# A hybrid decoder step on one core: the opening's transposes, weight splits and gate matmuls rearranged, and the sample state decayed by one ScalarE pass

## The reference

```python
h = rmsnorm(x, norm1_g)
z = h @ w_in                                   # 2048 x 16400
u, cg, bg, q, k, v, o, gif, g_a, g_b = split(z)
conv_out, sc = causal_dwconv(cg * u, sc0, w_shortconv)
a_out = bg * conv_out
gif = gif + b_if                               # 16 columns: 8 input gates, 8 forget gates
ig, lf = gif[:, :H], log_sigmoid(gif[:, H:])
hb, (c, n, m) = mlstm_sequence(qh, kh, vh, ig, lf, state0, first)
b_out = sigmoid(o) * hb
x = x + (sigmoid(g_a) * a_out + sigmoid(g_b) * b_out) @ w_out
up, fc = causal_dwconv(rmsnorm(x, norm2_g) @ w_up, fc0, w_ffconv)
x = x + (silu(up[..., D_FF:]) * up[..., :D_FF]) @ w_down
# for each sample row, in mlstm_chunk:
c_new = carry * c_prev + g * outer(k, v)       # 128 x 256 for each of 8 heads
```

## Time and profile before

| | us |
|---|---|
| median of 3 runs | 1738.02 |
| lowest and highest | 1737.58, 1740.27 |
| the profiled execution | 1736.41 |
| its span in the trace | 1734.7 |
| PE busy | 1720.7 (99%) |
| DVE busy | 1155.1 (67%) |
| ACT busy | 741.5 (43%) |
| POOL busy | 480.5 (28%) |

### The profile page before, as it was taken

The page is one execution under the profiler, slowest core; times in us unless marked ns, Lnnn a source line. Parts: engine busy times, 40 slices in busy tenths (PEclk is TensorE's granted clock), DMA queues, the critical chain, the costliest instruction groups (busy, mean ns, idle before and its releaser), DMA issues.

```text
span 1734.7 us, 37218 instructions
## 1 busy us (share of the span) xinstructions
PE 1720.7 (99%) x13803; PEld 1707.1 (98%) x13803; DVE 1155.1 (67%) x1775; ACT 741.5 (43%) x866; POOL 480.5 (28%) x473
## 2 busy tenths in 40 slices
PE   9999999999999999999999999999999999999997
PEld 7999999999999999999999999999999999999997
DVE  4674757557475765748677887777555777777554
ACT  6534334334433434443445454454433333334443
POOL 3541615234161523416111222222000222222000
PEclk9999999999999999999999999999999999999999
DMA  7877785877768588786665666666666666666653
GB/s 193 205 209 187 193 200 151 224 187 204 192 184 210 148 219 189 205 198 179 181 182 158 184 183 181 179 174 178 180 180 187 173 179 181 173 179 182 176 170 115
DMA packets 591287, 318.78 MB, mean 184 GB/s; under 512 B 16695, under 2 KB 585847, under 8 KB 589103
## 3 DMA queue, kind: packets, MB, share of 16 engines
q1 hardware_dynamic: 578999, 293.39, 62.8%
q10 hardware_dynamic: 11800, 21.88, 4.4%
q0 software_dynamic: 400, 2.20, 0.5%
HBM read 305.07 MB, written 12.78 MB: 183 GB/s over the span
## 4 chain that ended last, share of the span: by engine, by line
PE 98%; DVE 1%; DMA 0%; ACT 0%; issue 0%; SPq 0%; DVEq 0%
PE strip L1325 62%; PE strip L1330 31%; PE aux L1228 1%; PE aux L1422 1%; PE aux L1426 1%; PE aux L1395 0%; PE aux L1278 0%; PE strip L1261 0%; DMA x_tok<-in_x_prompt 0%; PE aux L1236 0%; PE strip L1271 0%; PE aux L1438 0%; DVE xl L916 0%; PE strip L1228 0%; ACT xh L637 0%
## 5 line engine op out<-in xcount | busy, mean ns | idle before, releaser
L881 DVE TENSOR_TENSOR w_lo<-w_raw,w_hi 128x1024 fp32r<-128x1024 f32 x556 | 713.4, 1285 | 378.5 <-ACT w_hi L620 375.9
L620 ACT ACTIVATE w_hi<-w_raw 128x1024 fp32r<-128x1024 f32 x560 | 592.1, 1060 | 849.5 <-PE strip L1330 815.4
L1325 PE MATMUL strip<-xh,w_hi 128*128 128x266 f32 (+2 forms) x3424 | 866.5, 287 | 0.0
L1325 PE MATMUL strip<-xl,w_hi 128*128 128x266 f32 (+2 forms) x3424 | 864.7, 286 | 0.0
L1325 PEld LDWEIGHTS strip<-xh,w_hi 128*128 128x128 f32 x3424 | 644.7, 188 | 0.3
L1325 PEld LDWEIGHTS strip<-xl,w_hi 128*128 128x128 f32 x3424 | 644.1, 188 | 0.0
L1330 PE MATMUL strip<-xh,w_lo 128*128 128x266 f32 (+2 forms) x3424 | 494.4, 286 | 0.0
L1330 PEld LDWEIGHTS strip<-xh,w_lo 128*128 128x128 f32 x3424 | 451.6, 188 | 0.0
L1325 PE MATMUL strip<-hh,w_hi 128*128 128x264 f32 x704 | 176.2, 286 | 0.0
L1325 PE MATMUL strip<-hl,w_hi 128*128 128x264 f32 x704 | 174.7, 283 | 0.0
L604 POOL TENSOR_TENSOR gg<-sg,cz 128x264 f32<-128x264 f32 x44 | 58.2, 1323 | 412.1 <-ACT sg L825 412.1
(11 more groups left out here) (287 smaller groups left out, 1267.4 us busy)
## 6 DMA issues: line engine op xcount, KB each, us to landing
w_raw<-in_w_in SPq DMA_DIRECT2D x256, 512.0 KB, 4.4
w_raw<-in_w_up SPq DMA_DIRECT2D x176, 512.0 KB, 4.1
w_raw<-in_w_down SPq DMA_DIRECT2D x64, 512.0 KB, 3.9
w_raw<-in_w_out SPq DMA_DIRECT2D x32, 512.0 KB, 4.3
w_raw<-in_w_down SPq DMA_DIRECT2D x32, 384.0 KB, 3.3
out<-c_st ACTq DMA_DIRECT2D x8, 1024.0 KB, 7.3
c_st<-in_state_mlstm_C ACTq DMA_DIRECT2D x7, 1024.0 KB, 11.3
rb<-scratch_rows ACTq DMA_DIRECT2D x8, 270.0 KB, 4.6
```

The costliest lines, as they stand in the source:

```text
L620: act.activation(w_hi[:, slot, :], w_raw[:, slot, :], ACT.Copy).then_inc(hi_done, 1)
L881: v.tensor_tensor(w_lo[:, slot, :], w_raw[:, slot, :], w_hi[:, slot, :].bitcast(f32), ALU.subtract).then_inc(lo_done, 1)
L1325: pe.matmul(bank[b][:, 0:c1 - c0], w_hi[:, slot, w], xt[:, k0 + k, c0:c1], start=(first and k == 0 and t == 0), stop=False)
```

## The change

It does the following.

- Transposes: each call of `turn_x` takes four feature blocks and does those of equal height together (four of row block 1, four of row block 0, four of the 24-row block; in later calls the 24-row ones first). The four single `warm` calls between transposes and the three behind them become six behind them. `x_bank` has six banks, `aux[0]` and `aux[1]` among them.
- First unit: ACT makes `w_hi` of unit 0 in two halves, the first before its copy of block 3. `first_hi` and `first_lo_part` are cut to pieces of four or two blocks and interleaved anew. DVE makes `w_lo` of unit 0, POOL those of units 2, 1 and 3.
- DVE makes `xl` of even blocks from the PSUM bank, and copies to `xres` after it.
- Gates: one stationary tile of 104 columns, `gws`, holds the high part in columns 0 to 39 and the low part in 64 to 103. Two matmuls for each block, 32 in all. DVE adds the two halves with one copy and one addition. `gws` lies where `v_t`, `v_tok` and `kg` are later.
- Norm factors: ACT's root and DVE's `refine` and `diag` come one unit earlier in their order.
- Loads: on SP's queue unit 1 goes ahead of the fourth quarter of x, and the first four units of v (4 to 7) stand at other places. Two DRAM to DRAM copies on POOL's queue move from the opening to behind head 0.
- Sample state: ACT multiplies all of `c_st` by the decay in one pass of 128x2048, after its step i = 13 (14 in head 0), and POOL's four multiplications for each head go.

```diff
-        x_bank = (bank[2], bank[3], aux[2], aux[3])
+        x_bank = (bank[2], bank[3], aux[2], aux[3], aux[0], aux[1])
@@ SP, first_front
                 load_x(2)
+                first_unit(0, 1, OQ)
                 load_x(3)
-                first_unit(0, 1, OQ)
                 first_unit(1, 1, OK)
                 sp.dma_start(gw[:, :, :], w_in[0].rearrange("(k p) n -> p k n", p=P)[:, :, OIF:OIF + 2 * H])\
                  .then_inc(gates_in, 16)
+                third_unit(0, OV, 0, first_lo, 1)
...
-                for s, c in enumerate((OV, OV + P)):
-                    load_strip(2 * (s + 2), 2 * (s + 2), w_in_v, c)
+                third_unit(2, OV + P, 0, first_lo, 2)
+                third_unit(1, OV, 1, lo_done, RING + 2)
+                third_unit(3, OV + P, 1, lo_done, RING + 4)
@@ POOL
-            for i, u in enumerate((0, 2)):
-                g.wait_ge(hi_done, i + 1)
+            g.memset(gws[:, :, :].bitcast(f32), 0.0).then_inc(gw_split, 1)
+            g.wait_ge(hi_done, 2)
+            g.wait_ge(first_lo, 1)
+            g.tensor_tensor(w_lo[:, 2, :], w_raw[:, 2, :], w_hi[:, 2, :].bitcast(f32), ALU.subtract)\
+             .then_inc(first_lo, 1)
+            for i, u in enumerate((1, 3)):
+                g.wait_ge(hi_done, i + 3)
                 g.tensor_tensor(w_lo[:, u, :], w_raw[:, u, :], w_hi[:, u, :].bitcast(f32), ALU.subtract)\
-                 .then_inc(first_lo, 1)
+                 .then_inc(lo_done, 2)
...
-                            g.tensor_tensor(c_p, c_p, dec_p, ALU.mult).then_inc(dec_done, 1)
                             g.tensor_tensor(kv[:, :, :], vg[:, :].unsqueeze(1).broadcast_to([P, 2, DV]),
                                             kw_p.unsqueeze(2).broadcast_to([P, 2, DV]), ALU.mult).then_inc(kv_ready, 1)
                             g.wait_ge(kv_ready, n * (JG // 2) + (jp + 1))
-                            g.wait_ge(dec_done, n * (JG // 2) + (jp + 1))
+                            if jp == 0:
+                                g.wait_ge(dec_done, n + 1)
@@ ACT
+                if k == 3:
+                    act.wait_ge(unit_landed[0], 16)
+                    act.activation(w_hi[:, 0, 0:KU * P // 2], w_raw[:, 0, 0:KU * P // 2], ACT.Copy).then_inc(half_hi, 1)
...
+                    if i == (14 if first else 13):
+                        act.wait_ge(vb_in, n * 32 + 32)
+                        if first:
+                            act.wait_ge(c_first_in, 16)
+                        else:
+                            act.wait_ge(c_in, n * 16)
+                        act.activation(c_st[:, :, :], c_st[:, :, :], ACT.Copy, scale=qkd_g[:, 2 * JG:2 * JG + 1])\
+                           .then_inc(dec_done, 1)
@@ DVE
+                src = x_bank[k % 6][:, 0:NT] if k % 2 == 0 else xres[:, k, :]
+                v.scalar_tensor_tensor(out=xl[:, k, :], in0=src, scalar=vecs[:, k:k + 1],
...
+                if k % 2 == 0:
+                    v.tensor_copy(xres[:, k, :], x_bank[k % 6][:, 0:NT]).then_inc(x_kept, 1)
...
+                        v.tensor_copy(gabs[:, :], aux[1][GL:GM, 0:NT]).then_inc(g_step, 1)
+                        v.wait_ge(g_step, 1)
+                        v.tensor_tensor(gz[:, :], aux[1][0:GR, 0:NT], gabs[:, :], ALU.add).then_inc(g_step, 1)
@@ PE
+                    for t, xt in enumerate((xh, xl)):
+                        mm = pe.matmul(aux[1][0:GM, 0:NT], gws[:, k, :], xt[:, k, :], start=(k == 0 and t == 0),
+                                       stop=(k == KT - 1 and t == 1))
...
-            for k in range(4):
-                turn_x(k, k + 1)
-                warm(1)
-            warm(3)
+            turn_x(0, 4)
+            warm(6)
             first_hi(0, 0, 4)
             turn_x(4, 8)
-            first_hi(0, 4, 8)
-            first_lo_part(0, 0).then_inc(unit_used, 1)
-            first_hi(1, 0, 8)
+            first_lo_part(0, 0, 4)
+            first_hi(1, 0, 4)
+            first_hi(0, 4, 6)
+            first_lo_part(0, 4, 8)
+            first_hi(0, 6, 8).then_inc(unit_used, 1)
+            first_lo_part(1, 0, 4)
             turn_x(8, 12)
-            first_lo_part(1, 0)
+            first_hi(1, 4, 8)
+            first_lo_part(1, 4, 8)
             turn_x(12, 16)
-            first_hi(0, 8, 16)
-            first_lo_part(0, 1).then_inc(unit_used, 2)
-            first_hi(1, 8, 16)
-            first_lo_part(1, 1).then_inc(unit_used, 1)
-            pe.wait_ge(gw_split, 6)
+            first_hi(0, 8, 12)
+            first_lo_part(0, 8, 12)
+            first_hi(1, 8, 12)
+            first_hi(0, 12, 16)
+            first_lo_part(0, 12, 16, True).then_inc(unit_used, 2)
+            first_hi(1, 12, 16)
+            first_lo_part(1, 8, 16, True).then_inc(unit_used, 1)
+            pe.wait_ge(x_kept, KT // 2)
+            pe.wait_ge(x_copied, KT // 2)
+            pe.wait_ge(gw_split, 5)
             gates(0, KT).then_inc(gz_done, 1)
```

More of the change, by code:

```diff
@@ L587, in _ @@
             back(0, first=True)
+            g.dma_start(s_sconv[0, :, 0, :], state_sconv[0, :, 1, :]).then_inc(moved, 16)
+            g.dma_start(s_fconv[0, :, 0, :], state_fconv[0, :, 1, :]).then_inc(moved, 16)
             with g.Fori(1, H) as n:
@@ L664, in front @@
                     step(n, HEAD_U, 0, i)
-                    if first and i == 1:
+                    if first and i == 0:
                         act.wait_ge(ms_done, 2)
@@ L941, in front @@
                     step(n, HEAD_U, 0, i)
+                    if first and i == 0:
+                        norm_rows()
                     if first and i == 3:
+                        v.wait_ge(gz_done, 1)
+                        v.tensor_copy(gabs[:, :], aux[1][GL:GM, 0:NT]).then_inc(g_step, 1)
+                        v.wait_ge(g_step, 1)
+                        v.tensor_tensor(gz[:, :], aux[1][0:GR, 0:NT], gabs[:, :], ALU.add).then_inc(g_step, 1)
                         v.wait_ge(r_spread, 1)
@@ L1242, in turn_x, with part @@
             def turn_x(lo, hi):
-                for k in range(lo, hi):
-                    if k % 4 == 0:
-                        pe.wait_ge(x_in[k // 4], 16 * 3)
-                    if k >= 4:
-                        pe.wait_ge(xl_done, k - 3)
-                    for j in range(3):
-                        r = P if j < 2 else TL
-                        mm = turn(x_bank[k % 4][:, j * P:j * P + r], x_tok[0:r, j, k * P:(k + 1) * P], r)
-                    mm.then_inc(x_turned, 1)
+                pe.wait_ge(x_in[lo // 4], 16 * 3)
+                if lo > 0:
+                    free = hi - len(x_bank)
+                    pe.wait_ge(xl_done, free)
+                    pe.wait_ge(x_kept, (free + 1) // 2)
+                    pe.wait_ge(x_copied, free // 2)
+                def part(k, j):
+                    n = P if j < 2 else TL
+                    return turn(x_bank[k % 6][:, j * P:j * P + n], x_tok[0:n, j, k * P:(k + 1) * P], n)
+                if lo == 0:
+                    for k in range(lo, hi):
+                        part(k, 1)
+                    pe.wait_ge(ends_in, 16 * 2)
+                    for k in range(lo, hi):
+                        part(k, 0)
+                    for k in range(lo, hi):
+                        part(k, 2).then_inc(x_turned, 1)
+                else:
+                    for k in range(lo, hi):
+                        part(k, 2)
+                    for k in range(lo, hi):
+                        part(k, 0)
+                        part(k, 1).then_inc(x_turned, 1)
             def first_hi(s, lo, hi):
@@ L1255, in first_hi @@
                 for k in range(lo, hi):
-                    if k % KU == 0:
+                    if s == 0 and k == 0:
+                        pe.wait_ge(half_hi, 1)
+                    elif k % KU == 0 or (s == 0 and k == 4):
                         pe.wait_ge(hi_done, 1 + s + 2 * (k // KU))
@@ L1260, in first_hi, with first_lo_part @@
                     for t, xt in enumerate((xh, xl)):
-                        pe.matmul(bank[s][:, 0:NT - c0], w_hi[:, 2 * s + k // KU, w], xt[:, k, c0:NT],
-                                  start=(k == 0 and t == 0), stop=False)
-            def first_lo_part(s, h):
+                        mm = pe.matmul(bank[s][:, 0:NT - c0], w_hi[:, 2 * s + k // KU, w], xt[:, k, c0:NT],
+                                       start=(k == 0 and t == 0), stop=False)
+                return mm
+            def first_lo_part(s, lo, hi, last=False):
                 c0 = M0 if s == 0 else 0
+                h = lo // KU
                 if h == 0:
@@ L1269, in first_lo_part @@
                     pe.wait_ge(lo_done, RING + 2 * (s + 1))
-                for k in range(KU):
-                    mm = pe.matmul(bank[s][:, 0:NT - c0], w_lo[:, 2 * s + h, k * P:(k + 1) * P], xh[:, h * KU + k, c0:NT],
-                                   start=False, stop=(h == 1 and k == KU - 1))
+                for k in range(lo, hi):
+                    pe.wait_ge(xh_done, k + 1)
```

(2 more changed lines are left out.)

92 lines of the change are left out of this document (44 added, 48 removed).

## The result

| us | before | after |
|---|---|---|
| median of the runs compared | 1739.14 (4 runs) | 1731.65 (4 runs) |
| lowest and highest | 1737.58, 1741.27 | 1731.25, 1731.97 |
| the profiled execution | 1736.41 | 1731.66 |
| its span | 1734.7 | 1729.6 |

The ratio is 0.995 [0.9938, 0.9962]: the changed kernel is faster, by half a per cent. The medians stand 7.5 us apart, the spans 5.1 us. The first is taken from few runs. A later comparison, with 10 runs of the changed kernel and 28 of the one before, gave 1730.61 and 1737.39 us, 0.9967 [0.9955, 0.998], that is 3.5 to 7.8 us of gain.

What follows compares the result with a forecast made beforehand. PE's own length, busy 99% of the span, was taken as the bound. Opening terms -1.1, -2.1, -1.1, -0.9, -2.05 and +0.6 gave -6.6 us: 1738.02 to 1731.4 us; 8-in-10 range 1729.4 to 1734.6.

Steps and rivals of the forecast that it cites:

- until the first real matmul: PE's opening: fewer transposes and constant matmuls ahead, so the first real matmul starts at 11.8 us, not 12.93; saves 1.1 us.
- three groups of transposes: The other three transpose groups in PE's opening take 1.45 us each instead of 2.16; saves 2.1 us (1.4 to 2.6).
- stretches that waited for xl and w_lo: Two stretches of PE's opening lose their waits: 1.1 us saved for `xl`, 0.9 us for `w_lo`.
- gates: Gate matmuls in PE's opening fall from 48 to 32 at 0.128 us each; saves 2.05 us.
- new wait for xl: DVE's odd-block `xl` slowed beside POOL's subtractions in the opening, 0 to 4 us, mostly slack; taken as +0.6 us.
- No cost: Unit 2's load in the opening lands at 12.5 us; ACT splits until 13.6, before PE wants it at 15.0.
- rival 1: In the opening DVE, held up by POOL, delays `xl` up to 4 us; 1733 us in the middle, 1734.8 worst; chance 0.14.
- Norm factors: Before PE's eleven transposes: root one unit earlier, `rbc` copied until 40.8 us, wanted at 41.4, 0.6 us left.
- Rival 3: TensorE's clock falls to 1.2 GHz in the opening from 7.26 us, costing about 3 us: 1734.4 us; chance 0.07.
- Decay: Sample state in each head: POOL loses 5.8 us, ACT gains a 1.91 us pass in idle time; taken as 0.
- Rival 4: ACT stands at the decay for a late `vg`, 2 us of PE wait for each head: 1747.4 us; chance 0.04.
- After unit 4: From unit 4 on nothing holds PE up, so the whole 6.6 us gained before it reaches the end.

Runs made afterwards that it cites:

- the second profile: The changed kernel, unchanged, run and profiled again beside more runs of the kernel before: 1730.61 us, ratio 0.9967.
- two kernels: Decay moved to ACT on the kernel before: 1736.69 us, 0.9998; decay put back on POOL in the changed kernel: 1731.28 us, 0.9969.

## Why the prediction was right, step by step

The forecast was 1731.4 us, and 1731.65 was measured. Part of that closeness is luck (later runs of the changed kernel have a median of 1730.61, also within the forecast). It started from a median of 3 runs that lay 1 us high. By its own profiled execution it forecast 1729.8 us and a span of 1728.1; the first profile gave 1731.66 and 1729.6, the second 1730.56 and 1728.5. The sum to unit 4, -6.65 us, was -4.87 in the first profile and -6.1 in the second. By its terms, in the first profile (its third and fifth rows take the kernel with all `xl` from PSUM as the one without a new wait):

| term | forecast | by the traces |
|---|---|---|
| until the first real matmul | -1.1 | -1.1 |
| three groups of transposes | -2.1 | -2.9 |
| stretches that waited for xl and w_lo | -2.0 | -1.1 |
| gates | -2.05 | -2.0 |
| new wait for xl | +0.6 | +2.2 |
| sum | -6.65 | -4.9 |

- **First matmul.** At 11.86 us against 11.8. Two misses cancelled: x landed 0.6 us later (7.88 us against 7.26), and from the first transpose on it took 3.98 us, not 4.55: the six calls took 2.6 us (9.26 to 11.86), not 3.0, and the transposes 1.4 us.
- **Transposes.** 1.2 us a group where 1.45 was forecast. Between 19.75 and 20.95 us twelve fit. In the group at 13.13 us the four of 24 rows with the change of height stand for 0.35 us, where 0.40 + 0.17 was forecast; two of them start 0.15 us ahead of the next two, so each takes about 0.075 us, less than the 0.10 us of the forecast and than the 0.107 us that stood beside it. The forecast's bounds, 1.4 to 2.6 us saved, didn't hold -2.9.
- **The stretches.** Where `xl` is never slow (all from PSUM), the opening up to unit 4 is 33.73 - 7.72 = 26.0 us. Its parts are 3.98 for the start, 96 x 0.128 = 12.3, three groups 3.6, gates 4.1 and nine transposes 1.0, together 25.0. So 1.0 us remains in slower first matmuls behind transposes. Before, the same sum is 5.67 + 12.3 + 6.5 + 6.1 + 1.0 = 31.6 of 40.94 - 7.26 = 33.7 us, 2.1 us over. The terms of 1.1 and 0.9 us counted all of that 2.1 as gained; 1.1 was. Which part of the new order gives it (the pieces in another sequence, six banks, POOL's `w_lo`, the moved loads) was not run by itself.
- **New wait for xl: the mis-sized term.** The opening of the first profile is 36.07 - 7.88 = 28.2 us, 2.2 us above that 26.0; PE's recorded waits for `xl` are 1.5 of it. In the second profile it is 35.04 - 7.42 = 27.6 us, 1.6 above. The forecast was 0.6. The 0.6 us between the two profiles is the landing of unit 2: ACT's split of it starts 5.83 us behind the first transpose in the first, 5.26 in the second. The mechanism, DVE with two SBUF operands beside POOL, was named with the right row (up to 1504 ns), but its place in time was set by the load of unit 2. "No cost" was wrong for that load: it landed at 13.69 and 12.65 us in the two profiles where 12.5 was taken from the earlier trace rows. ACT splits unit 2 ahead of block 4, so all `xh` and `xl` behind it move with the landing. This was rival 1 in part.
- **Gates.** 32 x 0.128 = 4.11 us at 104 columns, as forecast.
- **Norm factors.** The prediction had them as a matter of slack for `rbc`, and that held: `rbc` is copied from 40.41 to 40.84 us, and PE's transposes start at 43.27, 2.4 us later. It missed what the move is for. Without it DVE idles ahead of `w_lo` of unit 4, all that follows in its order comes later, `pre_exp` meets POOL's `pre_f`, and 20 us on PE waits 2.6 us for `v_t`. The gates alone bring nothing for that reason, and the whole change loses 4.6 us without it (2.9 us in the profiled pair). The forecast was right since the change contains the move, not since the step was understood.
- **Clock.** Rival 3 didn't happen: after, PE's records show 1.00 from 7 us on, with the six calls. Without the calls the clock does fall, from 12 us on and not from 7.26, for 3 to 4 us.

```profile
7.00:9.00 2.00, 1.12 (x10) 0.95 (x10) 0.00 (x0) 0.00 (x0) 0.00 (x0) 1.00 1.14 282
```

- **Decay.** No cost and no gain in the span, by two kernels. 1.99 us a pass against 1.91 forecast, in ACT's idle time. Rival 4 had no sign.
- **After unit 4.** 1693.5 us from there to the end of the span, 1693.8 before: the opening counts one to one.

## What to carry to other kernels

Where one engine is busy 99% of the span, sum what the edit takes from its own stream up to the first point where nothing holds it up, and then ask for each feeding engine what it does *in order* ahead of the result that PE needs next, and which instructions of two engines an earlier PE brings together; a shortened stage can come back as a wait 25 us later. A gain of grouping shows whole only where the next slowest supplier is out of the way. Read an instruction that takes three times its usual time beside another engine as a wait, and try another source for its operand before another place for it.

## What the runs showed of the hardware

- A DVE instruction with both tensors in SBUF (`xl` from `xres`, 128x280) took 1.57 to 1.66 us when it met a POOL subtraction of 128x1024, and ended 0.3 us after it (for one of them, 17.54 and 17.23 us); alone it takes 0.50. With one of the two in PSUM it took 0.50 us in all sixteen cases, ten of them beside the same POOL work. POOL, which had started first, took no longer (2.37 to 2.39 us). An operation of 8x8 took 1.83 us for 0.15 in the same way. The Trainium skill, "SBUF — State Buffer", section "SBUF: two separate sides", states it as an exclusive lock on a port pair that the two engines share, held for the whole instruction by whoever starts first; the trace agrees, since the long instruction ends right behind POOL's in each of these cases.
- Transposes of unequal height in turn cost: twelve in the order 128, 128, 24 rows take 2.09 us, grouped by height 1.2 us. The weight loader stands 0.17 us ahead of each change to 24 rows. The width of the moving operand changes along with the height, and which of the two counts isn't separated.
- PE's clock went to 1.2 GHz after PE had stood 2.6 us (gates alone) and after 2.4 us behind twelve transposes (no constant matmuls), and stayed there for 3 to 4 us; after another wait of 2.6 us it stayed at 2.4 GHz. What decides between them stays open.
- In one execution PE's first matmuls ran at half rate until 11.2 us (1.25 us for two instead of 0.72) while the granted clock was recorded as 1.00. The cause is open.
